# Forget bias formed inside the score products, and a router on four column groups, in a decoder layer on one core

## What is computed

```python
# four heads with forget gates ("FoX"), 64 wide, causal
log_f = log_sigmoid(fa + b_forget)            # (B, S, 4)
cum   = cumsum(log_f, axis=1)
s = q @ k.T * HEAD_DIM ** -0.5                # per head
s = s + (cum[t] - cum[s])                     # the forget bias
s = where(key_pos <= q_pos, s, -inf); p = softmax(s)

# router
logits = h @ w_router + b_router              # (256, 32)
top_vals, top_idx = top_k(logits, 4); gate = softmax(top_vals), scattered to 32 columns
# expert e: clamped SwiGLU of h @ w_e1[e] (1024 x 2048), times gate, @ w_e2[e] (1024 x 1024)
```

## Time and profile before

| | us |
|---|---|
| median of 3 runs | 1121.94 |
| lowest, highest | 1121.67, 1122.83 |
| profiled execution | 1121.48 |
| its span in the trace | 1119.7 |
| PE busy in the span | 1084.5 |
| DVE busy | 314.6 |
| ACT busy | 192.2 |
| POOL busy | 143.7 |

### The profile page before, as it was taken

How to read it: one execution, slowest core, us unless ns; L and a number is a source line. 1 busy time by engine, 2 the same in 40 slices (tenths; PEclk the granted TensorE clock), 3 DMA queues, 4 the chain that set the end, 5 groups by cost and what they waited for, 6 DMA issues and landing times.

```text
span 1119.7 us, 13613 instructions
## 1 busy us (share of the span) xinstructions
PE 1084.5 (97%) x5052; PEld 437.1 (39%) x5052; DVE 314.6 (28%) x664; ACT 192.2 (17%) x389; POOL 143.7 (13%) x298
## 2 busy tenths in 40 slices
PE   9999999999999999999999999999999999999998
PEld 6566756533333333333333333333333333233332
DVE  4577745222222222222222222222221211122222
ACT  1154425111111111111111111111111011111011
POOL 1042301201111111111111111110111111111100
PEclk9999999999999999999999999999999999999999
DMA  8814476799999999999999999999999999999995
GB/s 262 333 38 164 161 309 231 307 429 427 428 428 428 428 427 428 430 429 427 428 429 428 428 427 430 428 428 427 430 428 428 427 429 428 428 428 429 428 429 245
DMA packets 44023, 429.05 MB, mean 383 GB/s; under 512 B 6336, under 2 KB 13792, under 8 KB 19168
## 3 DMA queue, kind: packets, MB, share of 16 engines
q1 hardware_dynamic: 41648, 427.03, 91.3%
q10 hardware_dynamic: 2352, 1.71, 0.5%
HBM read 427.67 MB, written 1.05 MB: 383 GB/s over the span
## 4 chain that ended last, share of the span: by engine, by line
PE 68%; DMA 28%; DVE 2%; ACT 1%; issue 1%; DVEq 0%; SPq 0%
DMA ring<-in_w_e_dram 28%; PE banks L722 28%; PE banks L742 14%; PE banks L314 9%; PE banks L665 4%; PE banks L692 4%; PE banks L755 2%; PE banks L673 2%; PE banks L296 2%; PE banks L385 1%; PE banks L331 1%; PE banks L537 1%; PE banks L681 1%; PE banks L347 1%; PE banks L593 0%
## 5 line engine op out<-in xcount | busy, mean ns | idle before, releaser
L722 PE MATMUL banks<-ring,xg_T 128*64 128x512 f32 x2048 | 478.3, 599 | 24.7 <-DMA ring<-in_w_e_dram 23.5
L722 PEld LDWEIGHTS banks<-ring,xg_T 128*64 128x64 f32 x2048 | 135.7, 136 | 306.5 <-issue 254.3
L742 PE MATMUL banks<-ring,act_T 128*64 128x512 f32 x1024 | 232.9, 596 | 0.4 <-DVE act_T L1909 0.4
L1881 DVE TENSOR_TENSOR x_sb<-x_sb,banks 128x1024 f32<-128x1024 f32 x64 | 78.2, 1221 | 413.7 <-PE banks L692 382.9
L742 PEld LDWEIGHTS banks<-ring,act_T 128*64 128x64 f32 x1024 | 70.3, 137 | 132.5 <-issue 128.1
L1891 DVE TENSOR_TENSOR glu<-banks,b_T 128x512 f32<-128x512 f32 x32 | 22.1, 692 | 242.1 <-PE banks L755 242.1
L1069 POOL COPY picked<-slot_table 128x2 f32 (+1 forms) x32 | 6.1, 189 | 562.9 <-PE banks L681 562.9
L692 PE MATMUL banks<-y_sb,hot_gate_T 64*128 64x512 f32 x256 | 72.0, 640 | 0.8 <-ACT y_sb L1356 0.8
L1343 ACT COPY hidden<-banks 128x1024 f32<-128x1024 f32 x32 | 32.4, 1012 | 206.6 <-PE banks L722 206.6
L1329 ACT COPY xg_rows<-banks 128x512 f32<-128x512 f32 x33 | 19.3, 586 | 271.2 <-PE banks L665 271.2
L665 PE MATMUL banks<-h_sb,hot_slot 128*64 128x512 f32 x264 | 62.3, 592 | 0.0
(11 more groups left out here) (324 smaller groups left out, 773.0 us busy)
## 6 DMA issues: line engine op xcount, KB each, us to landing
ring<-in_w_e_dram SPq DMA_DIRECT2D x190, 2048.0 KB, 37.7
w_out_sb<-in_w_out_dram SPq DMA_DIRECT2D x1, 4096.0 KB, 13.2
ring<-in_w_e_dram SPq DMA_DIRECT2D x4, 1024.0 KB, 41.1
w_in_qk<-in_w_in_dram SPq DMA_DIRECT2D x1, 2048.0 KB, 24.3
w_mkv_sb<-in_w_mkv_dram SPq DMA_DIRECT2D x1, 2048.0 KB, 12.4
w_in_cq<-in_w_in_dram SPq DMA_DIRECT2D x2, 768.0 KB, 6.8
w_in_qc<-in_w_in_dram SPq DMA_DIRECT2D x1, 1536.0 KB, 26.0
w_in_kc<-in_w_in_dram SPq DMA_DIRECT2D x1, 1536.0 KB, 13.8
```

The lines of the kernel that those rows point to most:

```text
L722: ins = TE.matmul(PS[SLOTS * h:SLOTS * h + SLOTS, B_W1 + b, :], left, ring[slot][:, 2 * F * j + F * h + 512 * b:2 * F * j + F * h + 512 * ...
L742: ins = TE.matmul(PS[SLOTS * h:SLOTS * h + SLOTS, B_W2, :], actT[:, c % 4, c // 4, :], ring[slot][:, D * j + 512 * h:D * j + 512 * h + 512 ...
L1881: V.tensor_tensor(X[:, t, :], X[:, t, :], PS[:, first:first + 2, :].rearrange("p b n -> p (b n)"), ALU.add).then_inc(S("added"), 1)
```

## The change

It has three parts.

1. **Forget bias.** `logf` is copied 32 columns wide, so that one stationary tile of 128 columns holds four heads. One set of three products (`cum`) gives the running sums of all four heads, head h on partitions 32h to 32h+31, along the free axis. DVE's two instructions (`forget_leaves`) write two operands in which only two of a head's 32 rows are not zero: (c, 1) on the query side, (8, -8c) on the key side. A product over these 32 rows is 8 (c[t] - c[s]), which PE adds to the scores in PSUM, before DVE's scaling by 1/8. `score` then subtracts the plain causal mask. PE issues the three products ahead of the last of qc0's eight; DVE's two instructions stand in the middle of the Newton root of `roots("mla")`. The tiles with the zeros and ones (`ident_folded`, `ident_columns`) are made early on DVE.
2. **Router.** Each of the eight 128-row pieces of the contraction gives a 32x128 product; pieces k = 0 to 3 of a half go to column group k (partitions 32k to 32k+31). ACT copies the result (`router_parts`), and one product with `ident_folded` adds the four groups and turns the tile. `mem_out` is split, with `route(0)` between its halves. DVE's `choose(0)` stands in front of the root of x2_1, no longer interleaved with it.
3. **First one-hot rows.** They are compared with the ranks, which count from 1 (`rank_iota`), instead of with `slot_table`, which is now written behind them.

```diff
-    logfb = SCR[:, 0:1024].rearrange("p (t h m) -> p t h m", t=2, h=4)
+    logfb = SCR[:, 0:2 * P].rearrange("p (t h m) -> p t h m", t=2, h=FOX_H)
...
+            if names[0][0] == "f":
+                pe.wait_ge(S("mm_out"), left_no["cum"])
+                for a, b, q0, n in ((0, 128, 0, P), (128, 384, P, 2 * P)):
+                    for name, bank in zip(names, banks):
+                        r = slice(E * U_OF[name], E * U_OF[name] + E)
+                        ins = TE.matmul(bank[:, a:b], forget[r, 0, q0:q0 + P], forget[r, 1, 0:n], start=False, stop=a > 0)
...
-        project("qc", 0)
-        pe.wait_ge(S("logf_wide"), 1)
-        bank = into("cum")
-        TE.matmul(bank[:, 0:4], U[:, 0, :], logf[:, 0, :], start=True, stop=True)
...
-        for h in range(FOX_H):
-            bank = into(f"bias{h}")
-            TE.matmul(bank[:, 0:P], logfb[:, 0, h, :], U[:, 0, :], start=True, stop=True)
...
+            logs = [logfb[:, t].rearrange("p h m -> p (h m)") for t in range(NT)]
+            TE.matmul(bank[:, 0:P], logs[0], U[:, 0, :], start=True, stop=True)
+            TE.matmul(bank[:, P:2 * P], logs[0], U[:, 2, :], start=True, stop=False)
+            TE.matmul(bank[:, P:2 * P], logs[1], U[:, 0, :], start=False, stop=True).then_inc(S("mm_done"), 1)
...
+        for c in range(KC):
+            if c == KC - 1:
+                forget_sums()
+            ins = TE.matmul(bank[:, 0:384], rows(0)(c), win["qc"][:, c, :], start=(c == 0), stop=(c == KC - 1))
...
+            for half in range(2):
+                pe.wait_ge(S("turned_out"), turned_no[f"x2_{t}{half}"])
+                for k in range(4):
+                    c = 4 * half + k
+                    ins = TE.matmul(bank[E * k:E * k + E, 0:P], router_w[:, c, :], hT[:, c, t * P:(t + 1) * P],
+                                    start=(half == 0), stop=(half == 1))
+            ins.then_inc(S("turned"), 1)
+
+        def logits(t):
+
+            bank = into(f"router{t}")
+            pe.wait_ge(S("turned_out"), turned_no[f"parts{t}"])
+            TE.matmul(bank[:, 0:E], parts[:, t, :], spread[:], start=True, stop=True).then_inc(S("mm_done"), 1)
...
-        mem_out(1)
+        mem_out(1, 0)
         pe.wait_ge(S("router_scaled"), 1)
+        route(0)
+        mem_out(1, 1)
         turn_x_half("x2_", "mo", 1, 0)
-        route(0, 0)
+        logits(0)
         turn_x_half("x2_", "mo", 1, 1)
-        route(0, 1)
-        route(1, 0)
-        route(1, 1)
+        route(1)
+        logits(1)
...
             link(V.tensor_tensor(w, w, v, ALU.mult))
+            if amid:
+                amid()
...
+        def forget_leaves():
+
+            b = take("cum")[:, 0:T]
+            V.tensor_scalar(forget[:, 0, :], b, spread[:, 0:1], spread[:, 1:2], ALU.mult, ALU.add)
+            V.tensor_scalar(forget[:, 1, :], b, spread8[:, 0:1], spread8[:, 1:2], ALU.mult,
+                            ALU.add).then_inc(S("mm_out"), 1)
...
-        link(V.tensor_scalar(slot_of[:, :, 0:E], rank[:, :, 0:E], -1.0, None, ALU.add))
-        for t in range(NT):
-            ins = V.tensor_scalar(hot[:, t, :], iota[:, 0:SLOTS], slot_of[:, t, 0:1], y2[t], ALU.is_equal, ALU.mult)
+        for t in range(NT):
+            ins = V.tensor_scalar(hot[:, t, :], rank_iota[:], rank[:, t, 0:1], y2[t], ALU.is_equal, ALU.mult)
         ins.then_inc(S("hot_made"), 1)
+        V.tensor_scalar(slot_of[:, :, 0:E], rank[:, :, 0:E], -1.0, None, ALU.add)
```

More of the change, by code:

```diff
@@ L103, in build @@
     memT = at("mem_kT", [P, 2, T], 155648)
-    foxNB = at("fox_bias", [P, FOX_H, 384], 157696)
+    forget = at("forget_sums", [P, 2, T], 157696)
     SQ = at("head_squares", [P, 2, 3, T], 157696)
@@ L118, in build @@
     hotT = at("hot_gate_T", [P, T], Z + 19968)
+    spread = at("ident_folded", [P, E], Z + 18944)
+    spread8 = at("ident_columns", [P, 2], Z + 19072)
+    rank_iota = at("rank_iota", [P, SLOTS], Z + 19200)
+    parts = at("router_parts", [P, NT, P], Z + 19968)
     slot_of = at("slot_table", [P, NT, STEPS + 8], Z + 20992)
@@ L186, in build @@
     rowmax, rowsum, rowinv = stat[:, o:o + 4], stat[:, o + 4:o + 12], stat[:, o + 12:o + 16]
-    logf, fz, fa2, cumq, fe = (stat[:, o + 16 + 8 * k:o + 24 + 8 * k].rearrange("p (t h) -> p t h", t=2)
-                               for k in range(5))
+    logf, fz, fa2, fe = (stat[:, o + 16 + 8 * k:o + 24 + 8 * k].rearrange("p (t h) -> p t h", t=2)
+                               for k in range(4))
     x2_half = stat[:, o + 56:o + 58]
@@ L578, in mem_values, with mem_out, route @@
             ins.then_inc(S("mm_done"), 1)
-        def mem_out(t):
+        def mem_out(t, half):
             pe.wait_ge(S("o_left"), t + 1)
-            for half in range(2):
[L584 to L597, removed]
+            multiply(f"mo{t}{half}", lambda c: omT[:, c, t * P:(t + 1) * P],
+                     lambda c: wmo[:, c, 512 * half:512 * half + 512], 2)
+        def route(t):
+            bank = turn.next()
+            turned_no[f"parts{t}"] = turn.n
+            pe.wait_ge(S("turned_out"), turn.n - 4)
+            for half in range(2):
+                pe.wait_ge(S("turned_out"), turned_no[f"x2_{t}{half}"])
[8 more added lines that the diff above has]
+            TE.matmul(bank[:, 0:E], parts[:, t, :], spread[:], start=True, stop=True).then_inc(S("mm_done"), 1)
         merge("d", 0, 0)
@@ L1305, in _ @@
         turned_rows("x2_", 0)
+        leave("parts0", parts[:, 0, :], None, P)
         act.wait_ge(S("squared"), squares_n[0])
@@ L1313, in _ @@
             leave(f"x2_1{half}", hT[:, 4 * half:4 * half + 4, P:2 * P], 4, 512)
+        leave("parts1", parts[:, 1, :], None, P)
         act.wait_ge(S("logits_ready"), 1)
@@ L1420, in after_leaving, with roots @@
             dve.wait_ge(S("mm_out"), left[0])
-        def roots(name, parts):
+        def roots(name, spans, amid=None):
             assert REQ_NO[name] == req[0]
@@ L1427, in roots, with newton @@
             ss, v, y, w = (cols_of(kind, name) for kind in range(4))
-            for a, b, count in parts:
+            for a, b, count in spans:
                 ins = V.tensor_scalar(v[:, a:b], ss[:, a:b], 1.0 / count, EPS, ALU.mult, ALU.add)
             link(ins)
-            newton(v, y, w)
+            newton(v, y, w, amid)
             return y
-        def newton(v, y, w):
+        def newton(v, y, w, amid=None):
             v_bits, y_bits, w_bits = (ap.bitcast(I32) for ap in (v, y, w))
@@ L1627, in _ @@
         link(V.tensor_tensor(logf, fz, fe, ALU.subtract))
-        V.tensor_copy(logfb, logf.unsqueeze(3).to_broadcast([P, NT, FOX_H, P])).then_inc(S("logf_wide"), 1)
-        y_mla = roots("mla", [(0, 24, QK)])
+        V.tensor_copy(logfb, logf.unsqueeze(3).to_broadcast([P, NT, FOX_H, E])).then_inc(S("logf_wide"), 1)
+        def forget_leaves():
[3 more added lines that the diff above has]
+                            ALU.add).then_inc(S("mm_out"), 1)
+        y_mla = roots("mla", [(0, 24, QK)], forget_leaves)
         dve.sem_inc(S("mla_rooted"), 1)
         project("qc", 0)
[L1632 to L1637, removed]
-            V.scalar_tensor_tensor(out=foxNB[:, h, P:], in0=b[:, 0:2 * P], scalar=cumq[:, 1, h:h + 1],
-                                   in1=NBs[:, 0, P:], op0=ALU.subtract, op1=ALU.add).then_inc(S("mm_out"), 1)
-        after_leaving()
         score("f0")
@@ L1808, in _ @@
         add_out("mo11")
+        choose(0)
         squared("x2_1")
```

52 lines of the change are left out of this document (20 added, 32 removed).

## The result

| | before | after |
|---|---|---|
| median, 20 runs each | 1122.00 | 1125.14 |
| lowest, highest | 1120.15, 1124.25 | 1121.86, 1128.67 |
| profiled execution | 1121.48 | 1127.18 |
| its span | 1119.7 | 1125.4 |
| PE, DVE busy | 1084.5, 314.6 | 1087.2, 315.2 |

The changed kernel is slower: ratio 1.0028, 95% interval 1.0022 to 1.0035. The forecast was 1122.4, and the measured median lies just outside its range. What the median hides is that the runs of after fall into groups by the mean granted clock of TensorE over the span: six at 0.998 or more (mean 1122.98 us), eight at 0.997 (1125.18), six at 0.994 or 0.995 (1127.24). The first group lies 0.6 above the forecast, well inside its range; each further group is 2.1 to 2.2 us longer.

What follows compares the result with a forecast made beforehand. The end was taken to follow PE's first used slot, after which weight loads never pause. Forget bias +0.55, router +0.1 and ranks -0.2 summed to +0.45 us, so 1122.4 was expected, range 1119.6 to 1125.0.

Steps and rivals of the forecast that it cites:

- The term of the forget bias: From the forget sums to kc's projection: kc starts 0.55 us later (+0.1 to +1.3), POOL holding up DVE.
- The router term: Router up to `choose(1)`: +0.1 us, from -0.7 to +0.5.
- that rival: Router hand-offs become the bound: four ACT and PE exchanges 0.3 longer each, `choose(1)` about 0.5 later; 1122.9, chance 0.15.
- the one of four groups that don't run side by side: Router: the eight products take 1.78 us, mo11 comes 1.0 later than taken; +1.4, 1123.3, chance 0.08.
- The ranks' term: First one-hot rows: `slot_table` leaves the path, -0.2 us.
- TensorE falls to its lower level: Clock falls in the gaps before f1, slowing kc's records: +2.1 to +4.2 on top of +0.45, 1124.5 to 1126.6; chance 0.14.
- The other rival,: f0's division runs beside POOL's instruction, f1 ready 2.5 us earlier, kc -1.6; sum -2.2, 1119.7; chance 0.18.

Runs made afterwards that it cites:

- forget part alone: The kernel before with only the forget sums changed, router and ranks as before: 1124.80 us, ratio 1.0025; the profiled execution kept its clock.
- with the gap filled: The changed kernel with eight unread TensorE products between f0's and f1's transposes: 1122.12 us, ratio 1.0006.
- The kernel in which POOL waits: The changed kernel, with POOL waiting until f1's probabilities are divided before it touches the keys: 1119.86 us (ratio 0.9977), again 1119.93 (0.9990).
- the kernel before with the short filler: The kernel before with two filler products in place of four behind the counts of ranks: 1121.83 us, ratio 1.0002.

## Why the prediction was right and wrong

**The term of the forget bias.** Its chain happened almost step by step. The three sums stand one by one ahead of qc0's last product, in the order forecast. The pair of 32-row products takes 0.86 (68.25 to 69.11), as forecast. The division was to take about 2 us and to end with POOL's second wide instruction; it took 2.01. PE's wait for f1 was to be 2.1; it is 1.91. Without the clock the term measures +0.13 (copy to kc0, forget part alone), not +0.55. The bounds, from +0.1, held it. The sum was too high because it had DVE held again and again by POOL's small rotations. L1529 was not held (0.34), nor were f1's divisions (0.29, 0.34); what grew beside them was a rotation on POOL (L1002, 1.70 in place of 0.59). So f1 was ready 0.44 earlier than in the sum, and no gap of 0.5 opened ahead of f0.

**The router term.** +0.04 together with the ranks' part, +0.1 forecast alone. Sixteen records on four column groups took 0.58 from their start to the next product (197.61 to 198.19), 0.75 taken, 0.45 the lower bound. The mask met POOL's gain instruction as forecast (0.68). The hand-offs ended before `choose(1)`, so that rival is out, and so is the one of four groups that don't run side by side.

**The ranks' term.** Forecast -0.2, measured 0. The step that failed is that the one-hot rows were on the path because DVE's rows stood in line. PE's own rows were not looked at: before, its filler ended with the old rows (the gather follows MAX8 by 2.53 with four filler products and by 2.51 with two), so that new rows 0.23 earlier found PE still busy.

**The failed step is the clock.** The sum has no term for TensorE's clock: it counts the gap ahead of f1's transposes as a delay and nothing more, and leaves the lower level to a rival with a chance of 0.14. In the profile of after the fall behind that gap costs 3.3 us (1.34 ahead of kc0, 1.92 in it), and with the gap filled the median is back at 1122.12. The rival "TensorE falls to its lower level" had the place and the cause right, and its price too: 2.1 to 4.2, where the groups of runs lie 2.1 to 2.2 apart and the profile has 3.3. It named 1124.5 to 1126.6, and the median is 1125.14. A mean clock of 0.997 or less came in 14 of 20 runs. The argument for so little was that the trace of before "has no gap of that length in the middle of work". But that was a reason to have no opinion, not one against. The forecast's own first term made a gap of 2.1 us in a kernel that never had one, and the kernel before already spends filler products in three places. By these the rival deserved about even odds, and the range should have gone to 1127. The same holds for the router. There the text counted PE's shorter work as even, and did not ask what clock a stretch with 1.14 us of work in 2 us would be granted.

What it read the price from doesn't bear it, though. It took the records of rows 8, 0.59 us each, for the lower level. The trace has them at a granted clock of 1.00, and the same eight take 2.85 us in after. What 0.50 costs is shown by kc0 in after: about 3.9 of its 7.35 us lie at 0.50, and it takes 1.92 more than before, about half of 3.9. At that pace all sixteen records would have cost an estimated 5.3 us (their 5.33 again), not 4.2; the fall covered only a part of them. That the price fits is luck in part.

**The other rival,** that DVE is not held up, was worked out to 1119.7. The kernel in which POOL waits measures 1119.86 and 1119.93. The forecast had found both what the change was worth and what takes it away. That the totals meet is partly luck: the rival had 1.6 from this place and 0.6 from router and ranks; the place gave 2.0 and the other two gave nothing.

## What to carry to other kernels

When a change makes one engine's work shorter, follow the next instruction of the waiting engine to where it lands: here a division landed in another engine's long instruction, and one wait on that engine, whose results had time, was worth 5 us against the change as it stood. A gap that a sum prices at nothing may still cost more than its length in granted clock (here 1.91 us of waiting, 3.3 us behind it). Where a kernel spends filler products anywhere, give a new gap on TensorE of the length seen here (1.7 to 1.9 us) a fall of the clock as a term of the sum with a chance, and count in how many runs it happens rather than look at one profile. Before a step is taken off one engine's path, check that the engine which waits for it isn't busy with something else, its own filler included.

## What the runs showed of the hardware

**The clock's fall is a matter of chance.** With one and the same wait (1.91 us) one execution was granted 0.50 for 6.8 us and another 1.00 over the same products; over a kernel's runs a mean clock of 0.997 or less came in 14 of 20. The Trainium skill (TensorE: Matmul & The Clock Gate, Part 1) says that the count of slow products at a kernel's start varies from run to run with the gate's phase. The start of the kernels here agrees: the same eight records take from 2.85 to 5.49 us over the profiles. The falls in the middle of a kernel vary from run to run as well; that the phase sorts them, no run here shows.

**A few hundredths of a microsecond can be worth 0.4 us.** In the d stage one of DVE's divisions and POOL's scaling of the router's weights, which waits for a DMA, start almost together. In after:

```profile
134.12 0.70 DVE L1529 TENSOR_SCALAR scratch<-scratch,stat 128x256 f32<-128x256 f32 x1
```

```profile
134.04 0.64 POOL L1066 TENSOR_TENSOR w_router_sb<-w_router_sb,gain_columns 128x256 f32<-128x256 f32 x1 [2.32 <-DMA w_router_sb<-in_w_router_dram]
```

And before:

```profile
131.54 0.35 DVE L1497 TENSOR_SCALAR scratch<-scratch,stat 128x256 f32<-128x256 f32 x1
```

```profile
131.61 0.75 POOL L1039 TENSOR_TENSOR w_router_sb<-w_router_sb,gain_columns 128x256 f32<-128x256 f32 x1 [2.49 <-DMA w_router_sb<-in_w_router_dram]
```

DVE first by 0.07 us: 0.35, and kc0 to mo10 takes 113.01. POOL first by 0.08: 0.70, PE waits 0.25 for it, and the stretch takes 113.43 without the clock's share (115.35 less 1.92). It is no effect of the change, since the kernel before with the short filler shows it too (0.79, POOL 0.02 behind; 113.43). Three profiles of the sixteen have 113.0; the others have about 0.4 more, apart from what falls of the clock and waits add. A difference of that size between two profiles has to be looked for there before it is given to a change.
